# The head of a three-layer kernel: input halves counted apart, low-rank tables waited for apart, token differences made quarter by quarter

## What is computed

```python
c_act = jax.nn.silu(c)
shift, scale, gate = jnp.split(c_act @ ada_w + ada_b, 3, axis=-1)
h = _rmsnorm(x, g_pre) * (1.0 + scale[:, None]) + shift[:, None]
proj = h @ w_in                       # 26 column groups of 128
h_prev = _shift(h)
xw = h + (h_prev - h) * mu_w
xa = h + (h_prev - h) * mu_a
w = ... jnp.tanh(xw @ w1) @ w2 ...    # width 64
a = ... (xa @ a1) @ a2 ...            # width 64
```

## Time and profile before

| | |
|---|---|
| runs, us | 2131.95, 2130.07, 2134.81 (median 2131.95) |
| profiled execution | 2134.48 us, with a span of 2132.5 us |
| mean granted TensorE clock | 0.943 |
| TensorE busy (matmuls) | 1925.1 us, 90% |
| VectorE, ScalarE, GpSimd busy | 1198.6, 641.6, 99.7 us |
| HBM read | 146.32 MB, 70 GB/s over the span |
| the first 80 us by the chain | items 21.5%, quarters 13.1%, low-rank product 12.0%, sum of squares 11.3%, loads of x 9.6%, of the lora tables 8.5%, of ring slots 7.7% |

### The profile page before, as it was taken

One profiled execution on the slowest core, in us unless ns is written; L12 is line 12 of the kernel. 1 busy time (PEld: TensorE's weight loads), 2 busy tenths in 40 slices (PEclk: granted clock), 3 DMA queues, 4 the chain that ended last, 5 costly groups with the idle time before them and its releaser, 6 DMA issues.

```text
span 2132.5 us, 35201 instructions
## 1 busy us (share of the span) xinstructions
PE 1925.1 (90%) x15006; PEld 1645.0 (77%) x15006; DVE 1198.6 (56%) x2235; ACT 641.6 (30%) x1224; POOL 99.7 (5%) x53
## 2 busy tenths in 40 slices
PE   5999946997998877999999996997999999999997
PEld 2444435954997546999999996787866899999996
DVE  4004466414655664687775345799366477777423
ACT  2032221213212553322222221310377532222221
POOL 0000000100000000000000002132200000000000
PEclk8999967998999887999999998998999999999998
DMA  8220310010452000333233332143200133333331
GB/s 337 82 67 18 119 70 1 4 40 30 114 137 69 1 1 20 93 96 89 90 94 95 100 99 80 44 127 90 60 1 1 31 90 90 89 91 95 93 100 60
DMA packets 51291, 160.42 MB, mean 75 GB/s; under 512 B 8256, under 2 KB 9280, under 8 KB 51008
## 3 DMA queue, kind: packets, MB, share of 16 engines
q1 hardware_dynamic: 43648, 147.35, 22.4%
q10 hardware_dynamic: 7488, 10.82, 2.0%
HBM read 146.32 MB, written 2.10 MB: 70 GB/s over the span
## 4 chain that ended last, share of the span: by engine, by line
PE 80%; DVE 16%; issue 2%; ACT 1%; DMA 1%; ACTq 0%; SPq 0%; DVEq 0%
PE banks L471 17%; PE banks L472 16%; PE banks L473 16%; PE banks L1487 8%; PE banks L1643 3%; PE banks L1791 3%; PE banks L538 2%; DVE arena L1365 2%; DVE top L1364 2%; PE banks L592 2%; PE banks L516 1%; PE banks L528 1%; PE banks L564 1%; DVE stat L1128 1%; PE banks L583 1%
## 5 line engine op out<-in xcount | busy, mean ns | idle before, releaser
L471 PE MATMUL banks<-hn_hi,w_hi 128*128 128x264 f32 x2288 | 659.3, 288 | 30.4 <-DVE hn_lo L1044 14.2
L472 PE MATMUL banks<-hn_lo,w_hi 128*128 128x264 f32 x2288 | 654.3, 286 | 0.0
L473 PE MATMUL banks<-hn_hi,w_lo 128*128 128x264 f32 x2288 | 653.9, 286 | 0.0
L810 ACT ACTIVATE w_hi<-raw 128x1024 fp32r<-128x1024 f32 x207 | 219.3, 1061 | 896.3 <-PE banks L473 844.6
L471 PEld LDWEIGHTS banks<-hn_hi,w_hi 128*128 128x128 f32 x2288 | 437.0, 191 | 34.9 <-issue 20.3
L472 PEld LDWEIGHTS banks<-hn_lo,w_hi 128*128 128x128 f32 x2288 | 437.6, 191 | 0.1
L473 PEld LDWEIGHTS banks<-hn_hi,w_lo 128*128 128x128 f32 x2288 | 435.2, 190 | 0.0
L1038 DVE TENSOR_TENSOR w_lo<-raw,w_hi 128x1024 fp32r<-128x1024 f32 x181 | 221.6, 1225 | 200.4 <-ACT w_hi L810 200.4
L471 PE MATMUL banks<-a_hi,w_hi 128*128 128x264 f32 x704 | 199.6, 284 | 1.6 <-DVE u_in L1251 1.6
L472 PE MATMUL banks<-a_lo,w_hi 128*128 128x264 f32 x704 | 200.5, 285 | 0.0
L473 PE MATMUL banks<-a_hi,w_lo 128*128 128x264 f32 x704 | 199.6, 284 | 0.0
(11 more groups left out here) (343 smaller groups left out, 2641.7 us busy)
## 6 DMA issues: line engine op xcount, KB each, us to landing
raw<-in_weights SPq DMA_DIRECT2D x207, 512.0 KB, 3.6
ring<-in_weights SPq DMA_DIRECT2D x50, 512.0 KB, 5.4
arena<-arena ACTq DMA_DIRECT2D x144, 66.0 KB, 2.4
arena<-in_gate_w SPq DMA_DIRECT2D x8, 512.0 KB, 3.7
h<-in_xT SPq DMA_DIRECT2D x2, 1024.0 KB, 6.6
out_t<-h SPq DMA_DIRECT2D x4, 512.0 KB, 2.8
arena<-in_alibi SPq DMA_DIRECT2D x1, 1024.0 KB, 9.4
arena<-in_cosT ACTq DMA_DIRECT2D x2, 264.0 KB, 2.8
```

The lines of the kernel that those rows point to most:

```text
L471: mm(o, w[0][:, j, :], x[0][:, k, t], start=first, stop=False)
L472: mm(o, w[0][:, j, :], x[1][:, k, t], start=False, stop=False)
L473: ins_ = mm(o, w[1][:, j, :], x[0][:, k, t], start=False, stop=last)
L810: nc.scalar.activation(w_hi[:, j % SPLIT, :], raw[:, j % RAW, :], ACT.Copy).then_inc(S["w_hi_done"], 1)
```

## The change

The halves of x get a semaphore each, and ScalarE squares parts 0 to 3 when the first half is there. The table of columns is issued behind four ring slots. loraW is issued behind slot 15, not 17. lora2 counts on c_in, and TensorE waits for it ahead of line 1505, so that VectorE waits for loraW alone. VectorE makes the differences of a quarter behind the next quarter's affine step, and scales loraW when all differences are made. zb_d moves from mix to the front of the arena, where the gates lie later (agate, rgate, ggate), since ada_row is still in use when the first differences are made. The two memsets at the start count on one semaphore.

```diff
-        return mix[:, k, :]
+        return arena[:, P + k * T1:P + (k + 1) * T1]
...
-        for k in (0, 4):
-            sp.dma_start(h[:, k:k + 4, META:T2], ins["xT"][:, k:k + 4, :]).then_inc(S["x_in"], 16)
-        sp.dma_start(cols[:, :], ins["columns"]).then_inc(S["params_in"], 16)
+        for k, half in ((0, "x_in"), (4, "x_in_2")):
+            sp.dma_start(h[:, k:k + 4, META:T2], ins["xT"][:, k:k + 4, :]).then_inc(S[half], 16)
         for r in range(RING):
+            if r == 4:
+                sp.dma_start(cols[:, :], ins["columns"]).then_inc(S["params_in"], 16)
             sp.dma_start(ring[:, r, :], ins["weights"][r]).then_inc(w_loaded[r], 16)
...
-        for n in range(RING, S_IN1 + 2):
+        for n in range(RING, S_IN1):
             refill(n)
         sp.dma_start(loraW, ins["lora1"]).then_inc(S["lora_in"], 16)
-        for n in range(S_IN1 + 2, S_IN1 + 6):
+        for n in range(S_IN1, S_IN1 + 6):
             refill(n)
-        sp.dma_start(lora2, ins["lora2"]).then_inc(S["lora_in"], 16)
+        sp.dma_start(lora2, ins["lora2"]).then_inc(S["c_in"], 16)
...
         pe.wait_ge(S["in1_evac"], 2)
+        pe.wait_ge(S["c_in"], 32)
...
         act.wait_ge(S["c_in"], 16)
-        act.wait_ge(S["c_zero"], 1)
+        act.wait_ge(S["zero_cols"], 2)
         A(c_pad[:, :, 0:1], c_col.rearrange("p (k o) -> p k o", o=1), ACT.Silu).then_inc(S["c_silu"], 1)
-        act.wait_ge(S["x_in"], 32)
         for k in range(KT):
+            if k % 4 == 0:
+                act.wait_ge(S["x_in_2" if k else "x_in"], 16)
             A(hn1[:, k, 0:T1], h[:, k, META:T2], ACT.Square).then_inc(S["norm_sq"], 1)
...
-        V.memset(c_pad, 0.0).then_inc(S["c_zero"], 1)
+        V.memset(c_pad, 0.0).then_inc(S["zero_cols"], 1)
...
                                 ALU.mult, ALU.add).then_inc(S["hn_ready"], 1)
-        ve.wait_ge(S["lora_in"], 32)
+            if q:
+                ve.wait_ge(S["hn_ready"], k)
+                for j in (k - 2, k - 1):
+                    V.tensor_tensor(zb_d(j), h1[:, j, 0:T1], h1[:, j, 1:T1 + 1], ALU.subtract).then_inc(S["shift_diff"], 1)
+        ve.wait_ge(S["hn_ready"], KT)
+        for k in range(KT - 2, KT):
+            V.tensor_tensor(zb_d(k), h1[:, k, 0:T1], h1[:, k, 1:T1 + 1], ALU.subtract).then_inc(S["shift_diff"], 1)
+        ve.wait_ge(S["lora_in"], 16)
         for k in range(KT):
-            ve.wait_ge(S["hn_ready"], k + 1)
-            V.tensor_tensor(zb_d(k), h1[:, k, 0:T1], h1[:, k, 1:T1 + 1], ALU.subtract).then_inc(S["shift_diff"], 1)
             V.tensor_scalar(loraW[:, k, 0:64], loraW[:, k, 0:64], col("mu_w", k), None, ALU.mult)
             V.tensor_scalar(loraW[:, k, 64:P], loraW[:, k, 64:P], col("mu_a", k), None, ALU.mult).then_inc(S["lora_scaled"], 1)
```

More of the change, by code:

```diff
@@ L311, in build @@
     names = """key_dve key_pe key_act r_sums r_pointwise r_inputs r_norm_pe r_norm_dve r_norm_act slot_used params_in x_in consts_in meta_in out_stored dve_step act_step
-        c_in c_silu c_zero cond_in ada_copied ada_cols lora_in gate_in gate_used norm_sq norm_sum norm_var norm_std hn_ready shift_diff lora_scaled
+        c_in c_silu x_in_2 cond_in ada_copied ada_cols lora_in gate_in gate_used norm_sq norm_sum norm_var norm_std hn_ready shift_diff lora_scaled
         lora_done in1_evac zeroed zero_cols
```

## The result

| | before | changed |
|---|---|---|
| median, us | 2134.81 (2130.07 to 2136.37, 5 runs) | 2122.92 (2119.17 to 2124.42, 5 runs) |
| profiled execution, us (span) | 2134.48 (2132.5) | 2124.42 (2122.3) |
| mean granted clock | 0.943 | 0.942 |
| ratio of the runs, 95% interval | | 0.9942 [0.9927, 0.9956] |

The ratio is 12.4 us at 2134.8, with an interval of 9.4 to 15.6. The two profiled executions are 10.2 us apart in their spans.

The account below looks back on a forecast made before the run. TensorE, busy 90% of the span, bounds the kernel; until 63.08 us a relay of loads and short work does. Ending the low-rank product at 50.4 gives 12.7 us: 2131.95 - 12.7 = 2119.3 us, range 2115.5 to 2124.5.

Parts of the forecast that it names:

- the sum of squares: Sixteen TensorE matmuls on x at the kernel's start: begin at 7.48, end at 16.49 instead of 19.13, 2.64 us earlier.
- Quarter 1: Second of four ada matmul bursts: waits for the last initial ring slot, runs 20.1 to 21.9 us.
- Quarter 2: Third ada matmul burst: starts when its reloaded ring slots land, at 26.1 us instead of 28.76.
- The slots of quarter 3: Ring loads for the last ada matmul burst: follow without a gap and land at 31.2 us.
- VectorE's path from the columns of quarter 2: Affine steps, differences and loraW scalings ahead of the low-rank product: 9.3 us, from 34.15 to 43.45.
- The product: Low-rank product on TensorE, ending the head: starts at 43.6, takes 6.85 us instead of 9.56, ends at 50.4.
- Forecast A: Main forecast: full clock in quarters 2 and 3, low-rank product ends at 50.4, 12.7 us earlier; total 2119.3; 57%.
- Forecast B: Rival: clock falls before quarter 2, quarter 3 ends at 35.1, low-rank product at 52.5; 10.5 us gain, 2121.4; 24%.
- the clock stays full behind the 3.1 us gap: TensorE idle 23.0 to 26.1 us: full clock taken as likelier, so quarter 2 takes 1.82 us, not 3.64.
- rival D: Small-operation stages (266 to 373 us and others) meet the clock otherwise and run slower: about 2137 us; 3%.
- C: Rival: earlier sum of squares brings no earlier loads, quarter 3 still ends at 37.77; 7.9 us gain, 2124.1; 10%.
- E: Rival: most of the head's gain is absorbed later in the kernel, within 0.2%, about 2129 us; 3%.

Follow-up runs that it names:

- orders_back: The changed kernel with the loads in their old order (table of columns ahead of the ring slots, loraW behind slot 17); ratio 0.994 to the kernel before.
- after_third: The changed kernel unaltered, profiled a third time; ratio 0.9947 to the kernel before, low-rank product's end at 53.01 us.
- after_again: The changed kernel unaltered, profiled a second time; ratio 0.9944 to the kernel before, low-rank product's end at 50.68 us.
- warm: The changed kernel plus seven unused matmuls in the gaps ahead of quarters 1, 2 and 3; ratio 0.9941 to the kernel before.

## Why the prediction was right

**The sum, term by term.** The first half was there at 6.7, the sum of squares began at 7.51 (forecast 7.48) and ended at 16.18 (16.49; it took 8.67 us instead of 9.01, since its weight loads came 0.43 us apart from 10.94 on, 3.4 us behind the start, and before only 4.2 us behind it). TensorE came to the fifth part at 12.2, not at 10.9: a part is two recorded matmuls, and the forecast counted one, which made its margin too small and changes nothing else. Quarter 1 waited for the last initial slot until 20.40 (20.1). Quarter 2 started at 26.09 (26.1). This hit has some luck in it: the slots were free at 18.17, not 18.48, and the four loads took 7.92 us to quarter 2's start, not 7.64. The estimate from the Trainium skill (DMA: Bandwidth & Descriptors, "Anatomy of one DMA", 2.0 us plus bytes over 436 GB/s) had said 25.3; the page fits it to a single transfer issued by GpSimd, and here four were issued by SyncE. The slots of quarter 3 were there at 31.58 (31.2). VectorE's path from the columns of quarter 2 took 8.93 us, 36.12 to 45.05 (9.3; the scalings took 0.33 us a part, not 0.34, and the waits for its own results less than the 0.36 us allowed). TensorE's wait was 1.22 us (1.6). The product took 6.94 to 7.11 us (6.85).

Forecast A ended at 50.4; the changed kernel with a warm quarter 3 ended at 50.68, and orders_back at 50.27. Forecast B ended at 52.5; the two profiles of the changed kernel with a cold quarter 3 ended at 52.12 and 53.01. The 12.7 us of A is the distance from the end by the chain (63.08) to an end worked out from the distance between matmuls; from the same mark, 62.92, it would have been 12.5. The memsets were not done "8 us before anybody looks": ScalarE started its table load at 1.35, right behind the second one, in both kernels, so the merged counter does cost nothing, but not for the reason given.

**The clock, the step that was half wrong.** I weighed one gap, of 3.1 us ahead of quarter 2, and took the full clock as likelier. The gap ahead of quarter 1 stood in my own sum (18.3 to 20.1), and I did not ask what it does to the clock; in the first profile it came out at 2.29 us instead of 1.8, because the sum of squares ended 0.3 us sooner and the slot came 0.3 us later, and the clock fell just behind it. Quarter 2 turned out cold in all three profiles of the changed kernel, so the step "the clock stays full behind the 3.1 us gap" failed as it stands (the gap there was 3.42 and 3.50 us in the two where it came to one). It costs nothing when quarter 3 waits for loads; A and B differ only by quarter 3, and that one was cold in two of three. So B's time, at 24%, was at least as frequent as A's, though only in after_third did the clock fall where B has it, ahead of quarter 2, and stay down through quarter 3. The price that I gave the difference was 2.1 us; it is 1.4 to 1.8 (20.40 and 20.77 against 18.96). From the kernel before, the product's end moved by 10.8, 12.2 and 9.9 us in the three profiles, never by the 12.7 of A. The ratio's interval, 9.4 to 15.6 us, holds both A's 12.7 and B's 10.5; that its middle, 12.4, lies next to A's is luck, and does not show that A was the case.

**The later stages.** The head's gain reaches the end: from the second sum of squares on, the kernel before took 330.8 and 1300.7 us, the changed one 330.9 and 1300.5. The one stage that scatters otherwise is rival D's, the small operations and what follows them up to 500 us: 435.2 to 440.5 us, of which 1.7 us is the fall near 145 us. The stage up to line 604 had 325.8 us in two profiles of fourteen and 330.7 to 331.6 in the others. The stretch 700 to 720 us in the changed kernel and in after_again:

```profile
700.00:720.00 20.00, 17.19 (x86) 10.75 (x86) 11.15 (x26) 9.56 (x32) 0.00 (x0) 0.67 0.00 0
```

```profile
700.00:720.00 20.00, 17.15 (x117) 10.41 (x117) 12.51 (x31) 10.31 (x34) 0.00 (x0) 0.91 0.00 1
```

With the clock at 0.91 instead of 0.67, 117 matmuls go where 86 went. That the clock's falls make the two lengths fits this, but no run here held that stage's clock and nothing else; it stays argued. The forecast of 2119.3 and the median of 2122.92 differ for the most part by the base: the three runs that I took had a median of 2131.95, the five of the comparison have 2134.81, and over fifteen it is 2134.61. Whether the short form of that stage made the lowest of those three (2130.07) is not shown, for it has no profile.

**The rivals.** C (no earlier loads) fell: quarter 2 began 2.7 us earlier, and the DMA's idle stretch from 19.3 to 22.3 is gone. D (slower) and E (absorbed later) did not come.

## What to carry to other kernels

Before a wait is blamed on the load that it names, look which of the loads on its semaphore is the last, and who reads that one first: a load counted with another is waited for where the other is needed. Price a removed wait with the clock behind it: here 4.2 us of waiting took 2.5 us of half-speed matmuls with it. And where an early part is started sooner, follow the gain to the next load: with the halves alone quarter 3 ended 4.1 us earlier, and the product only 2.0, because the wait for lora2 still stood.

## What the runs showed of the hardware

- The granted clock fell while TensorE was already at work again, 0.7 us into quarter 1 and behind a gap of only 2.29 us (21.06, first profile of the changed kernel). Quarter 1 took 2.6 to 3.05 us, and so met a fall, in the four profiles whose gap ahead of it was 2.07 to 2.29 us, and 1.92 us in the six where it was 0.96 to 1.86 us (the ten without added matmuls). The gap is the shorter, the later the sum of squares ends (it took 8.67 us in the first profile of the changed kernel, 9.6 in after_again): an earlier end of the sum brought a colder quarter 1.
- Where quarter 3 waited for the last of its slots, the same 4 MB of refills let it start between 31.3 us (orders_back) and 32.9 us (warm), in kernels whose refills of the ring come in one order.
- A stage of some 330 us had two lengths, 5 us apart (325.8 and 330.7 to 331.6), with the same instructions; and a fall of the clock near 145 us came and went with edits 100 us ahead of it.
